# Finishing a cached row one unit earlier in the stick-breaking stage: gather ahead of the scores, weights and value groups moved up

## The chip, the cores and the metric

The kernel runs on one core of one Trainium2 chip. The metric is the device time of one launch in microseconds (µs), the median of several executions. The engines are called PE (TensorE), DVE (VectorE), ACT (ScalarE), POOL (GpSimd) and SP (SyncE, here a queue that only issues DMAs). Each engine runs its own list of instructions in order, and waits on semaphores for the others.

## The reference

One layer of a decoder mixes four parallel head groups, for a prompt of 1024 tokens and for 8 sample rows that each have 4096 cached tokens in 32 pages of 128. The part that matters here is group C, stick-breaking attention:

```
def stick_breaking(q, k, v, q_off, logit_bias):
    ...
        z = jnp.einsum('bqhd,bshd->bhqs', qi, kf) * Dh ** -0.5 + bias
        mask = kpos[None, :] < pi[:, None]
        l1mb = jnp.where(mask, jax.nn.log_sigmoid(-z), 0.0)
        after = lax.cumsum(l1mb, axis=3, reverse=True) - l1mb
        A = jnp.where(mask, jnp.exp(jax.nn.log_sigmoid(z) + after), 0.0)
        return jnp.einsum('bhqs,bshd->bqhd', A, vf)
...
        k_past = cache_sb_k[l][page_table].reshape(DB, past, SB_HEADS, SB_DIM)
        v_past = cache_sb_v[l][page_table].reshape(DB, past, SB_HEADS, SB_DIM)
```

For the prompt, queries and keys are the same 1024 tokens. For a sample row there is one query against the 4096 cached keys and values.

## The kernel before

The program is a chain of stages with a barrier between them. The change lies in the stage `stick_breaking_prompt`, which runs from about 110 to 565 µs of the profiled execution and does three things at once.

**The prompt.** The 8 heads are taken as 4 pairs, i = 0 to 3. A pair is cut in 12 pieces, u = 0 to 11, of one block of 128 queries by up to 512 keys: blocks 0 to 3 have one piece each (of 128, 256, 384 and 512 keys), blocks 4 to 7 two. The engines' loops run over g = 12 i + u; one turn is called a unit here. In unit g, PE multiplies the scores of piece g (L699, with the mask L705 on the diagonal), then a third of a projection tile (24 matmuls, L317; the last pair has only three such thirds, in its units 3 to 5), then it transposes the weights of piece g-2 (L717) and multiplies those of piece g-3 with the values (L732). ACT makes `keep` (L498) and `A` (L502) from the scores of each of the two heads; the second head's `keep` stands in ACT's list behind the first head's `A`, which needs a buffer that PE's transposes of unit g-2 set free. DVE scans `keep` to `left` (L567, L571) and multiplies it into `A` (L580).

**Tokens and tiles.** In units 2, 3 and 4 PE also transposes the new values, the sample row's tokens and the keys (L746, L773). DVE copies them out at the head of units 3 (`v_tok`, L623), 4 (`new_tok`, L628) and 5 (`k_tok`, L634), and PE's transposes of weights in these units wait for the copies, since they share the PSUM banks. At the head of unit 3 DVE also does `gate(i - 1, 1)` (L587), on which POOL's `store` (L669) waits.

**The cached rows.** Pair i also carries the sample row i. Its keys were multiplied with the query by POOL (L1966) and reduced by DVE (L1972) during the pair before; each POOL multiply takes a pair of pages, in a ring of four buffers. At the end of unit 11, ACT loads its exp/ln table, does `softplus_tail` (L1986 to L1990) and loads the sigmoid table again (L87), and DVE does `softplus` (L1994). Then, in the pair the row belongs to:

- PE `sum_pages` (L2002, L2003), the sums over the tokens of a page; unit 2
- DVE `exponents` (L2010 to L2018: a copy, a subtraction, 8 scans, a subtraction); unit 2
- ACT `weights` (L2023) between two table loads; unit 3
- PE `values.weigh` (L2096), 8 groups of 8 matmuls, one each at the end of the units 4 to 11 (`GROUPS`); SP loads the values for it (L2083), in a ring of four pairs of pages
- DVE `take_partial` (L2106) of the finished row; end of unit 0 of the next pair
- PE `gather` (L2112, 4 matmuls); unit 1 of the next pair, behind the projection third
- DVE `keep` (L2118); unit 1 of the next pair

SP's list is written by hand: loads of keys, values, weight tiles and stores of tokens alternate in a fixed order, and each waits there for its buffer.

Of the kernel before, what the change touches and what calls it, by code (L numbers as in the profile page):

```python
# [20 lines left out]
GT = GW // P  # L21
# [304 lines left out]
def stick_breaking_prompt(nc, ctx, k):  # L326
# [52 lines left out]
    values = PagedValues(ctx, nc, k, "cp", 0, GT, 4, PARTIAL, page_A)  # L379
# [1 line left out]
    Z, TURN, Y = k.bank[3:5], (k.bank[5], k.bank[2]), k.bank[6]  # L381
    quad = lambda bank: bank[:, :].rearrange("p (b t) -> p b t", b=4)
    REDUCES = (2, 1, 2, 1, 2, 1, 2, 1, 2, 1, 1, 0)
    GROUPS = (4, 5, 6, 7, 8, 9, 10, 11)
    V_TURNED, NEW_TURNED, K_TURNED = 2, 3, 4

    with nc.Block() as block:
# [76 lines left out]
        @block.scalar  # L464
        def _(act):
            keys.setup_scalar(act)

            def take(t, j, c):
                name, i = t
                columns = slice(c * CH, (c + 1) * CH)  # L470
                if name == "V":
                    if c == 0 and i:
                        act.wait_ge(tok_turned, 5 * i - 2)
                    stream.take(act, j, c, vT[:, columns], ACT.Copy)
                if name == "K":
                    if c == 0 and i > 1:
                        act.wait_ge(scored, 2 * NU * (i - 1))
                        act.wait_ge(tok_turned, 5 * (i - 1))
                    stream.take(act, j, c, kT[:, i % 2, columns], ACT.Copy)
                if name == "Q":  # L480
                    if c == 0 and i > 1:
                        act.wait_ge(scored, 2 * NU * (i - 1))
                    stream.take(act, j, c, qT[:, i % 2, columns], ACT.Copy, scale=SCORE_SCALE)
                if name == "G":
                    if i and c < 2:
                        act.wait_ge(mix_out[c], 16 * i)
                    if i and c == 2:
                        act.wait_ge(new_kept, i)
                    act.wait_ge(stream.projected, 3 * j + c + 1)
                    nc.scalar.activation(mix[:, columns], stream.bank(j, c)[:, 0:CH], ACT.Sigmoid).then_inc(gate_open, 1)  # L490

            def sigmoids(n):
                i, q, c = piece(n // 2)
                h, w = n % 2, wide(q, c)
                act.wait_ge(scored, n + 1)
                if n >= RK:
                    act.wait_ge(left_ready, n - RK + 1)
                nc.scalar.activation(keep[:, n % RK, W - w:W], Z[h][:, 0:w], ACT.Sigmoid, scale=-1.0,  # L498
                                     bias=minus[:, 2 * i + h:2 * i + h + 1]).then_inc(keep_ready, 1)
                if n >= RA:  # L500
                    act.wait_ge(A_turned, n - RA + 1)
                nc.scalar.activation(A[:, n % RA, 0:w], Z[h][:, 0:w], ACT.Sigmoid,  # L502
                                     bias=bias[:, 2 * i + h:2 * i + h + 1]).then_inc(sig_ready, 1)

            def take_turned(n):
                i, q, c = piece(n // 2)
                w = wide(q, c)
                act.wait_ge(A_turned, n + 1)
                if n >= RT:
                    act.wait_ge(weighted, n - RT + 1)  # L510
                nc.scalar.activation(AT[:, n % RT, 0:w], TURN[n % 2][:, 0:w], ACT.Copy).then_inc(AT_ready, 1)

            stream.split_hi(act, 0)
            stream.split_hi(act, 1)
            for j in range(3):
                for c in range(3):
                    take(tiles[j], j, c)
                stream.split_hi(act, j + 2)
            load_tables(nc, act, LN_EXP)
            keys.softplus_tail(act, 0)  # L520
            load_tables(nc, act, SIGMOID)
            act.wait_ge(bias_in, 16)
            act.wait_ge(minus_set, 1)
            act.wait_ge(ones_set, 1)
            for g in range(LAST + 3):
                i, u = g // NU, g % NU
                if g < LAST:
                    sigmoids(2 * g)
                    sigmoids(2 * g + 1)
                if g in chunk_of:  # L530
                    take(*chunk_of[g])
                if 2 <= g < LAST + 2:
                    take_turned(2 * g - 4)
                    take_turned(2 * g - 3)
                if u % 3 == 0 and 4 * i + 5 + u // 3 - 1 < len(tiles) and g:
                    stream.split_hi(act, 4 * i + 4 + u // 3)
                if u == 3 and i < GT:
                    load_tables(nc, act, LN_EXP)
                    act.wait_ge(values.weighed.sem, values.weighed.at(i, 0))
                    keys.weights(act, i)  # L540
                    load_tables(nc, act, SIGMOID)
                if u == NU - 1 and i + 1 < GT:
                    load_tables(nc, act, LN_EXP)
                    keys.softplus_tail(act, i + 1)
                    load_tables(nc, act, SIGMOID)

        @block.vector
        def _(dve):
# [65 lines left out]
            keys.softplus(dve, 0)  # L614
            for g in range(LAST + 3):
                i, u = g // NU, g % NU
                if u == V_TURNED + 1:
                    if i:
                        gate(i - 1, 1)
                        dve.wait_ge(v_out, 16 * i)  # L620
                    for q in range(2):
                        dve.wait_ge(tok_turned, 5 * i + q + 1)
                        nc.vector.tensor_copy(v_tok[:, 4 * q:4 * q + 4, :], quad(TURN[q])).then_inc(tok_taken, 1)  # L623
                if u == NEW_TURNED + 1:
                    dve.wait_ge(tok_turned, 5 * i + 3)
                    if i:
                        dve.wait_ge(new_out, 32 * i)
                    nc.vector.tensor_copy(new_tok[:].rearrange("p a b -> p (a b)"), TURN[0][0:NB, 0:2 * P]).then_inc(tok_taken, 1)  # L628
                if u == K_TURNED + 1:
                    if i:  # L630
                        dve.wait_ge(k_out, 16 * i)
                    for q in range(2):
                        dve.wait_ge(tok_turned, 5 * i + q + 4)
                        nc.vector.tensor_copy(k_tok[:, 4 * q:4 * q + 4, :], quad(TURN[q])).then_inc(tok_taken, 1)  # L634
                if u == HALF + 3:
                    gate(i, 0)
                if g < LAST:
                    products_left(2 * g)
                    products_left(2 * g + 1)
                    weights(2 * g)  # L640
                    weights(2 * g + 1)
                if g in chunk_of and chunk_of[g][0][0] == "G":
                    open_gate(chunk_of[g][1], chunk_of[g][2], i)
                if u % 3 == 0 and 4 * i + 4 + u // 3 < len(tiles) and g:
                    stream.split_lo(dve, 4 * i + 4 + u // 3)
                if u == 0 and i:
                    values.take_partial(dve, i - 1)
                if u == 1 and i:
                    values.keep(dve, i - 1)
                if u == 2 and i < GT:  # L650
                    keys.exponents(dve, i)
                if i < GT:
                    reduce_keys(i + 1, REDUCES[u])
                if u == NU - 2 and i + 1 < GT:
                    keys.add_bias(dve, i + 1)
                if u == NU - 1 and i + 1 < GT:
                    keys.softplus(dve, i + 1)
# [28 lines left out]
        def _(pe):  # L686
# [64 lines left out]
                    stream.chunk(pe, j, c)  # L751
            for g in range(LAST + 3):
                i, u = g // NU, g % NU
                if g < LAST:
                    scores(g)
                if g in chunk_of:
                    stream.chunk(pe, *chunk_of[g][1:])
                if u == 1 and i:
                    values.gather(pe, i - 1)
                if u == 2 and i < GT:  # L760
                    if i:
                        pe.wait_ge(values.kept.sem, values.kept.at(i, 0))
                    keys.sum_pages(pe, i)
# [11 lines left out]
                if i < GT and u == K_TURNED:  # L775
                    turn_tokens(kT[:, i % 2, :], tile_of["K", i], 5 * i + 3, g)
                if i < GT and u in GROUPS:
                    if u == GROUPS[0]:
                        pe.wait_ge(keys.A_ready.sem, keys.A_ready.at(i, 1))
                    values.weigh(pe, i, 2 * GROUPS.index(u))  # L780

# [38 lines left out]
class MemoryKeys:  # L820
# [14 lines left out]
    def quad(self):  # L835
        return self.bank[:, :].rearrange("p (b t) -> p b t", b=4)
# [1652 lines left out]
```

## Time and profile before

| | µs |
|---|---|
| Median of 3 executions | 1546.62 (1545.63 to 1547.21) |
| The profiled execution, its own time | 1546.62 |
| Its span in the trace | 1544.6 |
| Scores of pairs 0, 1, 2, 3 begin at (unit 0) | 151.8, 268.5, 375.0, 479.4 |
| PE busy | 1279.8, 83% of the span |
| DVE busy | 862.2, 56% |
| Mean granted clock of PE | 0.904 |

The profile is one execution. Busy shares are averages over the stages; a stage is read from its timelines, which give each instruction's start, its duration and, in brackets, the idle time ahead of it and what ended it. Busy time of DVE and POOL includes time in which an instruction had begun and stood still.

### The profile page before, as it was taken

To read this page: it belongs to the slowest core of one execution; us is meant where nothing else is said; L and a number is where in the kernel's file an instruction comes from. 1 tells how busy PE (TensorE), PEld (TensorE's weight loads), DVE (VectorE), ACT (ScalarE), POOL (GpSimd) and SP (SyncE) were. 2 spreads that over 40 slices of the span, in tenths; PEclk is the share of its full clock that TensorE was granted. 3 is DMA by queue.
4 is the path that set the end of the run, shared out by engine and by line. 5 is a ranking of instruction groups with operands and counts; after the bars stand their busy time and mean duration, and the time that the engine had idled before them with its cause. 6 is when DMAs were issued, how large, how long until landed. Compare 5 with 4: busy or idle time off the path is not lost. (4 is left out here: it accounts for less than half of the span.)

```text
span 1544.6 us, 23117 instructions
## 1 busy us (share of the span) xinstructions
PE 1279.8 (83%) x7719; PEld 1070.4 (69%) x7719; DVE 862.2 (56%) x1198; ACT 484.5 (31%) x902; POOL 358.3 (23%) x235
## 2 busy tenths in 40 slices
PE   3549589889798864998988899599999997797997
PEld 2539457767676543888888888488777776466885
DVE  4434779889886532759779496243434443324221
ACT  5311245435445531242232413231313131322110
POOL 0027544424330000736434354000000000000000
PEclk8679799999898986999999999798999997798999
DMA  4536657557473423655354642575646452543320
GB/s 137 164 91 213 199 183 248 169 176 248 141 228 110 146 81 103 209 172 177 104 170 140 206 150 71 163 217 154 205 143 215 141 178 70 177 136 109 109 81 28
DMA packets 200420, 237.89 MB, mean 154 GB/s; under 512 B 13539, under 2 KB 122434, under 8 KB 200298
## 3 DMA queue, kind: packets, MB, share of 16 engines
q1 hardware_dynamic: 196338, 224.61, 46.8%
q0 software_dynamic: 3968, 11.87, 2.1%
q8 instruction: 59, 0.97, 0.3%
q14 instruction: 55, 0.45, 0.1%
HBM read 215.88 MB, written 20.64 MB: 153 GB/s over the span
## 5 line engine op out<-in xcount | busy, mean ns | idle before, releaser
L1966 POOL TENSOR_TENSOR cp_keys<-cp_keys,cp_q 128x1024 f32<-128x1024 f32 x64 | 162.0, 2548 | 156.9 <-DMA cp_keys<-cache_sb_k 156.5
L1966 POOL TENSOR_TENSOR bp_keys<-bp_keys,bp_q 128x1024 f32<-128x1024 f32 x64 | 156.8, 2471 | 166.9 <-DMA bp_keys<-cache_sb_k 159.1
L248 PE MATMUL bank<-xh,b_w_hi 128*128 128x344 f32 x480 | 162.7, 339 | 31.4 <-DVE b_w_lo L231 27.2
L248 PE MATMUL bank<-xl,b_w_hi 128*128 128x344 f32 x480 | 157.8, 329 | 0.0
L248 PE MATMUL bank<-xh,b_w_lo 128*128 128x344 f32 x480 | 157.6, 328 | 0.0
L248 PE MATMUL bank<-xh,d_w_hi 128*128 128x344 f32 x384 | 131.1, 341 | 25.0 <-DVE d_w_lo L231 17.4
L317 PE MATMUL bank<-xh,c_w_hi 128*128 128x344 f32 x384 | 129.4, 337 | 17.0 <-DVE c_w_lo L303 17.0
L248 PE MATMUL bank<-xl,d_w_hi 128*128 128x344 f32 x384 | 126.2, 329 | 0.0
L317 PE MATMUL bank<-xl,c_w_hi 128*128 128x344 f32 x384 | 126.2, 329 | 0.0
L248 PE MATMUL bank<-xh,d_w_lo 128*128 128x344 f32 x384 | 126.1, 328 | 0.0
L317 PE MATMUL bank<-xh,c_w_lo 128*128 128x344 f32 x384 | 125.9, 328 | 0.0
L248 PEld LDWEIGHTS bank<-xh,b_w_hi 128*128 128x128 f32 x480 | 94.6, 197 | 34.7 <-ACT b_w_hi L226 28.0
L567 DVE TENSOR_TENSOR_SCAN c_left<-c_keep,ones 128x128 f32<-128x128 f32 (+3 forms) x64 | 98.7, 1557 | 33.1 <-ACT c_keep L498 32.9
L248 PEld LDWEIGHTS bank<-xh,d_w_hi 128*128 128x128 f32 x384 | 75.3, 196 | 53.2 <-issue 39.3
L2332 PE MATMUL bank<-o_w_hi,o_mix_hi 128*128 128x512 f32 x256 | 102.8, 401 | 10.5 <-DVE o_raw L2286 8.6
L502 ACT ACTIVATE c_A<-bank,c_bias 128x512 f32<-128x512 f32 (+3 forms) x96 | 55.8, 581 | 148.3 <-PE bank L717 148.3
L2332 PE MATMUL bank<-o_w_lo,o_mix_hi 128*128 128x512 f32 x256 | 101.6, 397 | 0.0
L2332 PE MATMUL bank<-o_w_hi,o_mix_lo 128*128 128x512 f32 x256 | 101.4, 396 | 0.0
L1972 DVE TENSOR_REDUCE bp_page_z<-bp_keys 128x16 f32<-128x1024 f32 x64 | 75.2, 1213 | 36.2 <-POOL bp_keys L1966 36.2
L248 PEld LDWEIGHTS bank<-xl,b_w_hi 128*128 128x128 f32 x480 | 94.4, 197 | 1.5 <-issue 1.4
L317 PEld LDWEIGHTS bank<-xh,c_w_hi 128*128 128x128 f32 x384 | 75.5, 197 | 27.1 <-issue 27.1
L248 PEld LDWEIGHTS bank<-xh,b_w_lo 128*128 128x128 f32 x480 | 94.0, 196 | 0.0
(381 smaller groups left out, 2600.1 us busy)
## 6 DMA issues: line engine op xcount, KB each, us to landing
cp_keys<-cache_sb_k SPq DMA_DIRECT2D x128, 256.0 KB, 2.9
cp_values<-cache_sb_v SPq DMA_DIRECT2D x128, 256.0 KB, 2.8
bp_keys<-cache_sb_k SPq DMA_DIRECT2D x128, 256.0 KB, 3.2
dp_values<-cache_sb_v SPq DMA_DIRECT2D x128, 256.0 KB, 2.9
b_w_raw<-w_in SPq DMA_DIRECT2D x20, 512.0 KB, 4.2
c_w_raw<-w_in SPq DMA_DIRECT2D x16, 512.0 KB, 5.1
d_w_raw<-w_in SPq DMA_DIRECT2D x16, 512.0 KB, 5.2
o_mix<-mix SPq DMA_DIRECT2D x8, 1024.0 KB, 5.8
```

The source lines that it names most:

```text
L248: last = self.nc.tensor.matmul(self.bank(j, c)[:, 0:self.width], w[:, s, k, :], x[:, k, c * self.width:(c + 1) * self.width], start=(k == ...
L317: last = self.nc.tensor.matmul(self.bank(j, c)[:, 0:self.width], w[:, k, :], x[:, k, columns], start=(k == 0 and m == 0), stop=(k == KT - ...
L502: nc.scalar.activation(A[:, n % RA, 0:w], Z[h][:, 0:w], ACT.Sigmoid, bias=bias[:, 2 * i + h:2 * i + h + 1]).then_inc(sig_ready, 1)
L567: nc.vector.tensor_tensor_scan(left[:, n % RL, W - w:W][:, ::-1], keep[:, n % RK, W - w:W][:, ::-1], k.ones512[:, 0:w], 1.0, ALU.mult, ALU ...
L1966: self.nc.gpsimd.tensor_tensor(self.keys[:, s], self.keys[:, s], q, ALU.mult).then_inc(self.scaled.sem, 1)
L1972: self.nc.vector.tensor_reduce(self.z[:, i % 2, :, 2 * r:2 * r + 2].rearrange("p h r -> p r h"), self.keys[:, r % self.ring].rearrange("p ...
L2332: last = nc.tensor.matmul(ACC[b][h][:, :], m[:, b, kk, :], w[:, kk, h * H:(h + 1) * H], start=(kk == 0 and n == 0), stop=(kk == KO - 1 and ...
```

## The change

The work on a cached row ends a unit earlier. `take_partial` goes to the head of unit 0 on DVE, ahead of its scans; `gather` goes to the head of unit 0 on PE, ahead of the scores; `keep` goes to unit 0. `sum_pages` and `exponents` move from unit 2 to unit 1, `weights` with its two table loads from unit 3 to unit 2. The eight value groups lie in units 3 to 6 and 8 to 11, unit 7 has none. SP's list is not changed. The loops also run three turns past the last unit, so the last row's `take_partial` and `gather` move with the others: ahead of the last transposes and weighings.

```
-    GROUPS = (4, 5, 6, 7, 8, 9, 10, 11)
+    GROUPS = (3, 4, 5, 6, 8, 9, 10, 11)
...
-                if u == 3 and i < GT:
+                if u == 2 and i < GT:
                     load_tables(nc, act, LN_EXP)
                     act.wait_ge(values.weighed.sem, values.weighed.at(i, 0))
                     keys.weights(act, i)
...
             for g in range(LAST + 3):
                 i, u = g // NU, g % NU
+                if u == 0 and i:
+                    values.take_partial(dve, i - 1)
                 if u == V_TURNED + 1:
...
                 if u == 0 and i:
-                    values.take_partial(dve, i - 1)
-                if u == 1 and i:
                     values.keep(dve, i - 1)
-                if u == 2 and i < GT:
+                if u == 1 and i < GT:
                     keys.exponents(dve, i)
...
             for g in range(LAST + 3):
                 i, u = g // NU, g % NU
+                if u == 0 and i:
+                    values.gather(pe, i - 1)
                 if g < LAST:
                     scores(g)
                 if g in chunk_of:
                     stream.chunk(pe, *chunk_of[g][1:])
-                if u == 1 and i:
-                    values.gather(pe, i - 1)
-                if u == 2 and i < GT:
+                if u == 1 and i < GT:
                     if i:
                         pe.wait_ge(values.kept.sem, values.kept.at(i, 0))
                     keys.sum_pages(pe, i)
```

## Rows read from the trace of the kernel before

**Rows 1.** Window, unit 7 of pair 1: length, busy PE, PEld, DVE, ACT, POOL; clock; DMA.

```profile
335.00:342.40 7.40, 7.34 (x52) 5.26 (x48) 7.40 (x9) 3.34 (x6) 1.59 (x3) 1.00 0.81 238
```

**Rows 2.** Waits of the stage, 150 to 560: who waited for whom, us, times, longest.

```profile
PEld bank L717 <- DVE c_new_tok L628: 17.3, 3, 6.4
```

**Rows 3.** Timeline of all engines where pair 0 ends and pair 1 begins.

```profile
268.54 0.49 PE L699 MATMUL bank<-c_kT,c_qT 64*128 64x128 f32 x4
...
271.22 0.42 DVE L1994 SCALAR_TENSOR_TENSOR cp_page_L<-cp_page_z,cp_page_soft 128x256 f32<-128x256 f32 x1
```

**Rows 4.** TensorE's timeline: unit 1 of pair 1, units 0 of pairs 2 and 3, unit 1 of pair 3.

```profile
279.80 0.95 PE L2112 MATMUL bank<-ones,cp_y_rows 128*128 128x1 f32 x8
...
374.97 0.49 PE L699 MATMUL bank<-c_kT,c_qT 64*128 64x128 f32 x4
...
479.35 0.49 PE L699 MATMUL bank<-c_kT,c_qT 64*128 64x128 f32 x4
...
485.53 1.22 PE L699 MATMUL bank<-c_kT,c_qT 64*128 64x256 f32 x4 [3.33 <-ACT c_A L502]
```

**Rows 5.** VectorE's and ScalarE's timelines at the borders of pairs 2 and 3.

```profile
378.21 0.42 DVE L1994 SCALAR_TENSOR_TENSOR cp_page_L<-cp_page_z,cp_page_soft 128x256 f32<-128x256 f32 x1
...
483.05 0.42 DVE L1994 SCALAR_TENSOR_TENSOR cp_page_L<-cp_page_z,cp_page_soft 128x256 f32<-128x256 f32 x1 [2.05 <-ACT cp_page_soft L1990]
...
485.10 0.38 ACT L502 ACTIVATE c_A<-bank,c_bias 128x128 f32<-128x128 f32 x1
```

**Rows 6.** VectorE's timeline, units 2 and 3 of pair 1.

```profile
291.63 0.42 DVE L2010 COPY cp_page_L<-bank 128x256 f32<-128x256 f32 x1
...
293.69 2.34 DVE L1972 TENSOR_REDUCE cp_page_z<-cp_keys 128x16 f32<-128x1024 f32 x2
295.95 0.68 DVE L587 TENSOR_TENSOR c_mix<-bank,c_mix 128x512 f32<-128x512 f32 x1
...
297.74 11.63 DVE L567 TENSOR_TENSOR_SCAN c_left<-c_keep,ones 128x512 f32<-128x512 f32 x2
```

**Rows 7.** GpSimd's timeline, 284 to 307.

```profile
284.42 2.39 POOL L1966 TENSOR_TENSOR cp_keys<-cp_keys,cp_q 128x1024 f32<-128x1024 f32 x1 [8.09 <-DMA cp_keys<-cache_sb_k]
...
297.86 9.30 POOL L1966 TENSOR_TENSOR cp_keys<-cp_keys,cp_q 128x1024 f32<-128x1024 f32 x4
```

**Rows 8.** TensorE's timeline, units 2 to 4 of pair 1; the last row unit 4 of pair 2.

```profile
287.80 0.38 PE L2002 MATMUL bank<-cp_page_L,from_here 128*128 128x256 f32 x1
288.01 0.59 PE L2003 MATMUL bank<-cp_page_L,ones 128*128 128x256 f32 x2
...
300.97 0.37 PE L773 MATMUL bank<-ident,c_kT 128*8 128x128 f32 x1 [2.06 <-ACT c_AT L511]
...
313.62 1.54 PE L717 MATMUL bank<-ident,c_A 128*128 128x128 f32 x6 [5.12 <-DVE c_new_tok L628]
...
420.04 1.54 PE L717 MATMUL bank<-ident,c_A 128*128 128x128 f32 x6 [6.11 <-DVE c_new_tok L628]
```

**Rows 9.** The end of the stage: TensorE's timeline, then VectorE's.

```profile
552.47 1.12 PE L717 MATMUL bank<-ident,c_A 128*128 128x128 f32 x8 [0.29 <-ACT c_AT L511]
...
554.53 1.05 PE L2112 MATMUL bank<-ones,cp_y_rows 128*128 128x1 f32 x8
...
553.68 0.69 DVE L2106 TENSOR_TENSOR cp_y_rows<-bank,cp_own 128x512 f32<-128x512 f32 x1
```

**Rows 10.** TensorE's value groups that waited for a load: pair 1 unit 9; pair 3 unit 8.

```profile
357.50 1.04 PE L2096 MATMUL bank<-cp_values,c_page_A 128*8 128x512 f32 x8 [1.00 <-DMA cp_values<-cache_sb_v]
...
537.92 1.07 PE L2096 MATMUL bank<-cp_values,c_page_A 128*8 128x512 f32 x8 [2.65 <-DMA cp_values<-cache_sb_v]
538.93 2.08 PE L699 MATMUL bank<-c_kT,c_qT 64*128 64x512 f32 x4
```

**Rows 11.** Window over the end of unit 3 and most of unit 4, pair 1; columns as above.

```profile
299.90:306.70 6.80, 5.73 (x22) 5.11 (x23) 6.80 (x1) 5.76 (x9) 6.80 (x4) 0.50 0.46 156
```

More of the change, by code:

```diff
@@ L383, in stick_breaking_prompt @@
     REDUCES = (2, 1, 2, 1, 2, 1, 2, 1, 2, 1, 1, 0)
-    GROUPS = (4, 5, 6, 7, 8, 9, 10, 11)
+    GROUPS = (3, 4, 5, 6, 8, 9, 10, 11)
     V_TURNED, NEW_TURNED, K_TURNED = 2, 3, 4
@@ L536, in _ @@
                     stream.split_hi(act, 4 * i + 4 + u // 3)
-                if u == 3 and i < GT:
+                if u == 2 and i < GT:
                     load_tables(nc, act, LN_EXP)
@@ L616, in _ @@
                 i, u = g // NU, g % NU
+                if u == 0 and i:
+                    values.take_partial(dve, i - 1)
                 if u == V_TURNED + 1:
@@ L646, in _ @@
                 if u == 0 and i:
-                    values.take_partial(dve, i - 1)
-                if u == 1 and i:
                     values.keep(dve, i - 1)
-                if u == 2 and i < GT:
+                if u == 1 and i < GT:
                     keys.exponents(dve, i)
@@ L753, in _ @@
                 i, u = g // NU, g % NU
+                if u == 0 and i:
+                    values.gather(pe, i - 1)
                 if g < LAST:
@@ L757, in _ @@
                     stream.chunk(pe, *chunk_of[g][1:])
-                if u == 1 and i:
-                    values.gather(pe, i - 1)
-                if u == 2 and i < GT:
+                if u == 1 and i < GT:
                     if i:
```

## The prediction

> **What bounds the kernel now.** I read the page first, then the waits of the stage, then the timelines of its borders. The page makes TensorE the busiest engine. In an undisturbed unit the reader is to see it busy for 7.34 of 7.40 µs at the full clock [rows 1], with VectorE occupied as long, part of it standing still. So the stage goes by TensorE, except where something stops it. The timelines show two such kinds of place in each pair.
>
> The first is unit 4. TensorE stands still for 5.12 µs in pair 1 and 6.11 µs in pair 2, and each time it is VectorE's copy of the new tokens that releases it [rows 8]; the waits give 17.3 µs for this wait over three pairs [rows 2]. VectorE is late because of unit 3: two scans of 512 take 11.63 µs, and beside them lie four multiplies of GpSimd in one piece, 297.86 to 307.16 [rows 6, 7]. VectorE gets on only when GpSimd pauses. GpSimd has four at once because its list waited for VectorE's gate at 295.95. From the gate to the end of TensorE's stall is 313.62 - 295.95 = 17.7 µs, of fixed steps; in pair 2 it is the same to 0.1. So in pairs 1 and 2 the time of the gate sets the time of all that follows. Its own time follows from TensorE's unit 2 and VectorE's work there.
>
> The second is not seen yet. At the border of two pairs TensorE runs on into unit 0 at 268.54, 374.97 and 479.35, while VectorE is still at `softplus` of the new row, which ends at 271.64, 378.63 and 483.47 [rows 3 to 5]. VectorE is 3.1 to 4.1 µs behind, because ScalarE's two table loads stand ahead of that instruction. Nobody suffers from it today.
>
> **The change part by part.**
>
> *Gather at the head of unit 0.* PE can't score before it has gathered, gather waits for `take_partial`, and that is behind `softplus`. After the end of `softplus` come 0.69 for `take_partial`, 0.16 to the first matmul of gather and about 0.9 for gather [rows 9], less a little overlap on VectorE: 1.7 µs. The scores of unit 0 then start at 271.64 + 1.7 = 273.3 instead of 268.54 (4.8 late), at 380.3 instead of 374.97 (5.4 late) and at 485.2 instead of 479.35. Behind gather are queued the scores, the projection third, the transposes and so all that ScalarE and VectorE get. The delay is not taken up on the way: units 0 to 2 are paced by TensorE's transposes, which ScalarE's second `keep` waits for. In pair 3 there is almost no projection, and unit 1 waited for ScalarE until 485.53 anyway [rows 4]. There, 0.9 for the scores and about 1.2 for ScalarE's four small sigmoids (0.38 each, overlapping) [rows 5] follow 485.2: unit 1 at 487.3, some 1.7 late.
>
> *Gather out of unit 1, the page sums in.* 0.95 leaves and 288.60 - 287.80 = 0.80 comes [rows 4, 8]: no change for unit 1.
>
> *Page sums and exponents out of unit 2.* The sums stood ahead of the transposes that the second scan hangs on: 0.8 earlier. The exponents took 293.69 - 291.63 = 2.06 of VectorE ahead of the gate [rows 6]. So the gate comes up to 2.9 earlier after the start of unit 2, and by the fixed 17.7 so does the end of the stall. Against it: in unit 1 the exponents would run about 8.4 to 10.5 µs after its start (275.06 for pair 1), and a multiply of GpSimd starts at 284.42, 9.4 after it [rows 7]. It can hold scans up to 2.4 µs, of which VectorE's later wait for `keep` takes up all but about 0.7. I take 2.5, between 2.2 and 2.9.
>
> The SBUF page of the Trainium skill ("two separate sides") says that VectorE and GpSimd share a port pair as an exclusive lock, held for the whole instruction by the one that starts first. The rows agree that it is all or nothing, but not on the length: the first scan begins 0.12 ahead of the multiplies and lasts through four of them. By one instruction of lock the stall of unit 4 would hardly be there.
>
> *Weights with table loads to unit 2.* Some 3 µs of ScalarE now lie ahead of its first `keep` of unit 3, about 1 µs more than it was idle there. VectorE wants that `keep` only after gate and copies, which hide it: nothing. If that cover went, about 1 µs a pair.
>
> *A value group in unit 3, none in unit 7.* The group, 1.0 µs [rows 10], lies ahead of the stall of unit 4, in its cover, in pairs 0 to 2. Pair 3 has no such stall, so +1.0. In unit 7 TensorE would wait for ScalarE's last `A` anyway: 0, and in the short units of pair 3 -0.5. SP's loads of values wait for the groups and come earlier for all but the last two, which ends waits of 1.00 in pair 1 and 2.65 in pair 3, and behind the latter the scores that ran at the low clock (2.08 for 1.13) give 0.9 [rows 10]. The waits in unit 11 lie ahead of the new stall and give nothing.
>
> *The end.* Gather now stands ahead of the last transposes of weights. It can't start before 554.53, as `take_partial` is still VectorE's next work at 553.68; the transposes that ran at 552.47 begin near 555.45: 3.0 late, less the 0.9 that gather no longer takes further on: +2.1 [rows 9]. The last gate, store and stage end follow.
>
> *Clock.* TensorE stands still for some 3.8 µs at each border. After an idle of 2.06 in unit 3 the granted clock was 0.50, the level of 1.2 GHz, from 299.9 to 306.7 [rows 8, 11]. Such a stretch on dense work costs half its length, at most 3.4; part of it falls in the idle itself. I take 1.7 for borders 1 and 2, bounds 0 and 3.4. At border 3 the clock was low already. The page "TensorE: Matmul & The Clock Gate" of the Trainium skill (Part 1) has the array fall to half rate after idling; the rows agree, and by that rule the new idle is not free, which speaks against the change.
>
> *Sum.* Pair 0: 0, as its unit 3 waits for keys that SP sends late, which the change doesn't move. Pair 1: 4.8 - 2.5 - 1.0 + 1.7 = +3.0. Pair 2: 5.4 - 2.5 + 1.7 = +4.6. Pair 3: 1.7 - 0.8 (sums out of unit 2) + 1.0 - 0.5 - 2.65 - 0.9 + 2.1 = -0.1. In all +7.5: 1546.6 + 7.5 = 1554.1. The profiled execution took 1546.62, as the median does, with a span of 1544.6.
>
> **Rivals.**
>
> *A: the border gets worse.* Loads come earlier, so GpSimd's multiplies move too. If one falls on VectorE's scans in unit 11, `softplus` and with it gather come 2.4 µs later. For it: GpSimd has multiplies near each of these borders. Against: today none of them delays `softplus`. Over two or three borders +5 to +7: near 1560.
>
> *B: it evens out.* The clock doesn't fall, the exponents meet no multiply, and pair 0 gives up to 2.9 as well since its exponents leave unit 2 too. 1554.1 - 3.4 - 0.8 - 2.9 = 1547.0. Against: each border's wait is hard.
>
> *C: the scan of unit 3 escapes.* The collision hangs on 0.12 µs. If the first scan gets through before GpSimd's four multiplies, the two stalls of 5.12 and 6.11 go: 1554.1 - 11.2 = 1542.9, faster. It decides from the point where the scan starts one length (1.2 µs) ahead. For it: VectorE is less loaded. Against: gate, copies, store and scan follow one another exactly as before, so both move together.
>
> **How the numbers follow.** My forecast's own range is 1554.1 - 3.4 - 0.8 = 1549.9 to 1554.1 + 3.4 + 0.6 = 1558.1. Chances: forecast 0.52, A 0.18, B 0.19, C 0.11. The range leaves out C and the top of A: 1546 to 1561. A measurement of this kernel tells 0.2%, about 3 µs, from no change: slower is the forecast and A, 0.70; within it B, 0.19; faster C, 0.11.
>
> **What would show it.** TensorE waiting for VectorE's `take_partial` ahead of gather, 3.5 to 4.5 µs at each of three borders, and the clock at half behind it; the gate 10.4 to 11.1 µs after unit 2's start instead of 13.3; the stall of unit 4 still there, with scans of some 11 µs; no waits for values in pair 3; gather ahead of the last transposes. I am wrong if TensorE reaches gather no earlier than VectorE is done, or if the piece of four multiplies breaks up.

## The result: slower by 1.2%, more than twice what was forecast

| | Before | Changed |
|---|---|---|
| Median, µs | 1546.35 (1545.63 to 1547.21, 4 runs) | 1566.54 (1564.60 to 1567.64, 4 runs) |
| Ratio, 95% interval | | 1.0118 [1.0096, 1.0142] |
| Span of the profile | 1544.6 | 1561.4 |
| Next stage's first matmul (L248) | 572.8 | 585.6 |

The changed kernel was measured once more, beside the kernel before on the same chip (e10): 1567.11 against 1546.82, ratio 1.0106 [1.0066, 1.0146]. The forecast was 1554.1 with a range up to 1561.

In the waits of the stage, 150 to 571, the wait for the partial row takes 24.4 µs in all, where the kernel before had 0.2; the columns are the time waited, how often, and the longest:

```profile
PEld bank L2112 <- DVE cp_y_rows L2106: 24.4, 4, 9.3
...
PE bank L2112 <- DVE cp_y_rows L2106: 20.7, 4, 8.4
```

These are four waits of TensorE (and of its weight loads, PEld) ahead of gather, for VectorE's `take_partial`: at the three borders of two pairs and at the end of the stage. This is the wait that was forecast, but longer. The timeline of all engines at the border of pairs 0 and 1 shows it, and answers to [rows 3]:

```profile
264.89 1.04 PE L2096 MATMUL bank<-cp_values,c_page_A 128*8 128x512 f32 x8
...
265.39 2.46 DVE L571 TENSOR_TENSOR_SCAN c_left<-c_keep,c_left,ones 128x513 f32<-128x513 f32 x2
...
267.67 5.09 POOL L1966 TENSOR_TENSOR cp_keys<-cp_keys,cp_q 128x1024 f32<-128x1024 f32 x2 [4.94 <-DMA cp_keys<-cache_sb_k]
267.77 5.55 DVE L580 TENSOR_TENSOR c_A<-c_A,c_left 128x512 f32<-128x512 f32 x2
...
273.24 0.41 DVE L1994 SCALAR_TENSOR_TENSOR cp_page_L<-cp_page_z,cp_page_soft 128x256 f32<-128x256 f32 x1
273.57 0.68 DVE L2106 TENSOR_TENSOR cp_y_rows<-bank,cp_own 128x512 f32<-128x512 f32 x1
...
274.31 1.87 PE L2112 MATMUL bank<-ones,cp_y_rows 128*128 128x1 f32 x8 [8.37 <-DVE cp_y_rows L2106]
...
276.10 0.80 PE L699 MATMUL bank<-c_kT,c_qT 64*128 64x128 f32 x4
```

The reader is to see three things. TensorE has done its last group at 265.93 and idles 8.37 µs. VectorE's two multiplies of `A` (L580) take 5.55 µs where they take 1.27 alone, beside two multiplies of GpSimd, the first of which starts 0.1 µs ahead of them: this is 4.3 µs for VectorE and, since it would have had to wait for ScalarE a little anyway, 3.7 µs for gather. And gather itself takes 1.87 instead of 0.95 [rows 4]; the granted clock is at its lower level there (0.50 from 274.31 to 276.10). The window over most of unit 0 behind it, with the mean granted clock as the seventh value (0.58), then DMA:

```profile
276.10:283.70 7.60, 7.60 (x33) 7.35 (x33) 0.42 (x1) 0.37 (x1) 0.00 (x0) 0.58 0.13 46
```

Unit 0 of pair 1 takes 9.40 µs (276.10 to 285.50) instead of 6.52. TensorE's timeline at border 3, where no multiply of GpSimd is near, shows the wait at its shortest, 4.72:

```profile
489.44 1.04 PE L2096 MATMUL bank<-cp_values,c_page_A 128*8 128x512 f32 x8
495.20 1.87 PE L2112 MATMUL bank<-ones,cp_y_rows 128*128 128x1 f32 x8 [4.72 <-DVE cp_y_rows L2106]
497.00 0.80 PE L699 MATMUL bank<-c_kT,c_qT 64*128 64x128 f32 x4
...
498.21 1.93 PE L717 MATMUL bank<-ident,c_A 128*128 128x128 f32 x8
...
501.52 0.70 PE L699 MATMUL bank<-c_kT,c_qT 64*128 64x256 f32 x4
```

The gains came as forecast. VectorE's timeline of units 2 and 3 of pair 1, against [rows 6], and TensorE's stall, against [rows 8]; unit 2 began at 293.09:

```profile
301.88 2.34 DVE L1972 TENSOR_REDUCE cp_page_z<-cp_keys 128x16 f32<-128x1024 f32 x2
304.13 0.68 DVE L587 TENSOR_TENSOR c_mix<-bank,c_mix 128x512 f32<-128x512 f32 x1
...
305.92 11.65 DVE L567 TENSOR_TENSOR_SCAN c_left<-c_keep,ones 128x512 f32<-128x512 f32 x2
```

```profile
321.82 1.54 PE L717 MATMUL bank<-ident,c_A 128*128 128x128 f32 x6 [4.62 <-DVE c_new_tok L630]
```

The gate comes 11.04 after the start of unit 2 instead of 13.32; from the gate to the end of the stall it is 17.7 again, with the two scans at 11.65, as good as unchanged (11.63).

### The profile page after: what moved, and what is told of

Its sections match the earlier page's. It is cut to its first block and busy times, and to the rows that moved or that the text cites. A ratio compares the mean times of both kernels' runs of the same rounds, so it can differ in the third digit from the quotient of the medians.

```text
span 1561.4 us, 23117 instructions
## 1 busy us (share of the span) xinstructions
PE 1282.6 (82%) x7719; PEld 1072.4 (69%) x7719; DVE 857.7 (55%) x1198; ACT 484.5 (31%) x902; POOL 359.5 (23%) x235
## 5 line engine op out<-in xcount | busy, mean ns | idle before, releaser
L248 PE MATMUL bank<-xh,b_w_hi 128*128 128x344 f32 x480 | 163.6, 341 | 31.3 <-DVE b_w_lo L231 27.2
L248 PE MATMUL bank<-xl,b_w_hi 128*128 128x344 f32 x480 | 158.5, 330 | 0.0
L248 PE MATMUL bank<-xh,b_w_lo 128*128 128x344 f32 x480 | 157.8, 329 | 0.0
L248 PE MATMUL bank<-xh,d_w_hi 128*128 128x344 f32 x384 | 130.7, 340 | 26.1 <-ACT d_w_hi L226 18.4
L248 PE MATMUL bank<-xl,d_w_hi 128*128 128x344 f32 x384 | 125.7, 327 | 0.0
L248 PE MATMUL bank<-xh,d_w_lo 128*128 128x344 f32 x384 | 125.7, 327 | 0.0
L248 PEld LDWEIGHTS bank<-xh,b_w_hi 128*128 128x128 f32 x480 | 94.9, 198 | 34.6 <-ACT b_w_hi L226 28.0
L248 PEld LDWEIGHTS bank<-xh,d_w_hi 128*128 128x128 f32 x384 | 74.9, 195 | 54.2 <-issue 40.4
L2332 PE MATMUL bank<-o_w_hi,o_mix_hi 128*128 128x512 f32 x256 | 103.0, 402 | 10.5 <-DVE o_raw L2286 8.6
L567 DVE TENSOR_TENSOR_SCAN c_left<-c_keep,ones 128x128 f32<-128x128 f32 (+3 forms) x64 | 79.1, 1257 | 44.2 <-ACT c_keep L498 44.1
L248 PEld LDWEIGHTS bank<-xl,b_w_hi 128*128 128x128 f32 x480 | 94.9, 198 | 1.6 <-issue 1.5
L248 PEld LDWEIGHTS bank<-xh,b_w_lo 128*128 128x128 f32 x480 | 94.6, 197 | 0.0
```

The lines of the kernel that those rows point to most:

```text
L248: last = self.nc.tensor.matmul(self.bank(j, c)[:, 0:self.width], w[:, s, k, :], x[:, k, c * self.width:(c + 1) * self.width], start=(k == ...
L567: nc.vector.tensor_tensor_scan(left[:, n % RL, W - w:W][:, ::-1], keep[:, n % RK, W - w:W][:, ::-1], k.ones512[:, 0:w], 1.0, ALU.mult, ALU ...
L2332: last = nc.tensor.matmul(ACC[b][h][:, :], m[:, b, kk, :], w[:, kk, h * H:(h + 1) * H], start=(kk == 0 and n == 0), stop=(kk == KO - 1 and ...
```

## The experiments

Each profile is read by the starts of the scores (L699). With `take_partial` behind `softplus`, gather never started sooner than 12.5 µs after the start of unit 11; that is called the floor. "Stage end" is the next stage's first matmul less its 572.8 in the kernel before; the times have that kernel beside them on the same chip.

| | Gather starts after start of unit 11, borders 1, 2, 3 | Stage end | Ratio of times, 95% interval |
|---|---|---|---|
| Changed | 16.1, 13.1, 12.5 | +12.8 | 1.0118 [1.0096, 1.0142] |
| Changed again (e10) | 13.6, 17.4, 12.5 | +16.0 | 1.0106 [1.0066, 1.0146] |
| e1 gather behind the third | inside unit 0 | +0.6 | 1.0013 [0.9990, 1.0036] |
| e2 gather only | 14.4, 12.5, 12.5 | +13.9 | 1.0118 [1.0082, 1.0154] |
| e3 last gather back | 13.5, 13.4, 12.5 | +8.6 | 1.0077 [1.0046, 1.0108] |
| e4 delay, kernel before | | +11.1 | 1.0078 [1.0048, 1.0108] |
| e5 gather at end of unit 0 | inside unit 0 | -17.2 | 0.9932 [0.9909, 0.9955] |
| e5 again (e12) | inside unit 0 | -6.3 | 0.9946 [0.9927, 0.9966] |
| e6 e5, partial before softplus | inside unit 0 | -14.0 | 0.9926 [0.9898, 0.9954] |
| e7 e5, weights and groups back | inside unit 0 | -9.3 | 0.9980 [0.9957, 1.0003] |
| e8 the wait filled | 16.2, 17.9, 12.5 | +17.7 | 1.0065 [1.0044, 1.0086] |
| e9 keys behind values | 12.5, 12.5, 12.5 | +9.7 | 1.0060 [1.0035, 1.0084] |
| e11 before again | | -1.2 | 0.9998 [0.9980, 1.0015] |

**e1: is it the place of gather?**

```
                     stream.chunk(pe, *chunk_of[g][1:])
+                if u == 0 and i:
+                    values.gather(pe, i - 1)
```

(and it goes from ahead of the scores.)

> The changed kernel, but in unit 0 TensorE does the scores and the projection third first and gathers behind them; VectorE's take_partial stays at the head of unit 0, the page sums, exponents, weights and value groups stay moved up. Theory (the border): what makes the changed kernel slow is TensorE standing still ahead of unit 0 for VectorE's take_partial. Then the stalls of borders 1 and 2 go (scores of unit 0 about 1 us or less behind the end of unit 11 instead of 10.2 and 7.1 us), the earlier gates stay, and the kernel is 4 to 8 us faster than the kernel before, some 25 us faster than the changed one; pair 3 and the end of the stage, which have no third in unit 0, keep most of their loss. Rival (the moved groups, weights and exponents cost the time themselves): it stays above the kernel before by 10 us or more.

The loss went, 12 µs at the stage's end against the changed kernel's first profile, but the kernel before was not beaten, where 4 to 8 µs were expected. The profile shows why: at border 2 the wait only moved. Gather began 8.64 after the scores of unit 0, with the third done at 4.69, since VectorE was held by GpSimd once more, and unit 0 took 12.95 µs. In pair 3 there is no third in unit 0 and gather still stood ahead of the transposes; counted from the start of unit 0, unit 1 came 4.1 later. The theory of the border holds; a third is too little cover. TensorE's gather at border 2:

```profile
380.82 1.05 PE L2112 MATMUL bank<-ones,cp_y_rows 128*128 128x1 f32 x8 [3.95 <-DVE cp_y_rows L2106]
```

**e2: the gather alone.** The kernel before with `take_partial`, `gather` and `keep` moved as in the change, nothing else.

> The kernel before with only take_partial, gather and keep moved to unit 0, take_partial and gather at its head; page sums, exponents, weights and value groups as before. Theory (the border): all of the loss and none of the gains, so slower than the changed kernel: 20 to 25 us above the kernel before. The border's wait of pair 1 is some 2 us shorter than in the changed kernel if GpSimd's multiplies fall on VectorE's unit 11 only because the value groups and with them SP's loads come earlier. Rival (moved groups and exponents cost the time): 0 to 6 us above the kernel before.

It is as slow as the whole change, with groups, exponents and weights where they were: the rival is out. It was not slower than the whole change as expected, 16 µs by the medians instead of 20 to 25. At border 1 gather starts at 14.4, 1.7 sooner than in the changed kernel's first profile but beyond the floor of 12.5, though no load moved. Here `softplus` itself (L1994, 0.42 alone) took 2.38 beside a multiply of GpSimd that began 0.25 ahead of it:

```profile
268.66 4.83 POOL L1966 TENSOR_TENSOR cp_keys<-cp_keys,cp_q 128x1024 f32<-128x1024 f32 x2 [5.66 <-DMA cp_keys<-cache_sb_k]
...
268.91 2.38 DVE L1994 SCALAR_TENSOR_TENSOR cp_page_L<-cp_page_z,cp_page_soft 128x256 f32<-128x256 f32 x1 [0.20 <-ACT cp_page_soft L1990]
```

So the collision is possible without earlier loads. How often it comes with them and without is counted where the prediction is answered below.

**e3: the end of the stage.** The changed kernel with `gather` at `g == LAST` back behind `weigh`.

> The changed kernel with the last row's gather alone back where it was at the end of the stage: behind the transposes and weighings of the turn after the last unit. Theory: the end of the stage gets back what the gather and the low clock behind it took there, so 3 to 5 us faster than the changed kernel. Rival: the end of the stage is set by something else, within 1 us of the changed kernel.

From the scores of the last unit to the end of the last weighing it is 11.2 µs again (556.71 to 567.95), where the changed kernel takes 16.4 (555.82 to 572.17). The changed kernel's timeline:

```profile
562.01 1.53 PE L2112 MATMUL bank<-ones,cp_y_rows 128*128 128x1 f32 x8 [2.25 <-DVE cp_y_rows L2106]
563.40 1.95 PE L717 MATMUL bank<-ident,c_A 128*128 128x128 f32 x8
565.28 1.98 PE L732 MATMUL bank<-c_AT,c_v_tok 128*64 128x128 f32 x16
567.18 1.99 PE L717 MATMUL bank<-ident,c_A 128*128 128x128 f32 x8
```

and with the last gather back:

```profile
560.94 1.12 PE L717 MATMUL bank<-ident,c_A 128*128 128x128 f32 x8 [0.30 <-ACT c_AT L511]
561.99 1.09 PE L732 MATMUL bank<-c_AT,c_v_tok 128*64 128x128 f32 x16
563.01 1.05 PE L2114 MATMUL bank<-ones,cp_y_rows 128*128 128x1 f32 x8
563.92 1.07 PE L717 MATMUL bank<-ident,c_A 128*128 128x128 f32 x8
```

From the scores of the last unit to the next stage it is 24.7 µs, against 29.8 and 28.5 in the two profiles of the changed kernel: 5.1 and 3.8 less, where 3 to 5 were expected; by the ratios the kernel is 4 to 6 µs faster than the changed one. Of the 5.1 the wait and the place of gather are some 2, and the rest goes with the low clock, at which gather, transposes and weighings took up to 1.99 for 1.12; this split is an estimate from the rows above.

**e4: do the stages behind care when they start?** Seven memsets of VectorE behind the last gate of the kernel before.

> The kernel before with seven VectorE memsets of 128x2052 (1.8 us each) behind the last gate of the stick-breaking stage; nothing else changed and the output is the same. It asks where the some 4 us come from that the changed kernel loses behind this stage, in stages whose code is the same. Theory (they depend on the instant at which they start): the later stages also take 1 to 5 us more or less than in the kernel before. Rival (they do not): from the next stage's first matmul on, all is later by one constant, about 9 us, within 0.5 us.

The next stage began 11.1 later, the last matmul only 9.2: from one to the other 959.1 µs, against 961.0. That is 1 to 5 µs of difference, as the theory had it, but e11 and e12 below show that two profiles of one kernel can differ there by more; so e4 does not show that the start is the cause.

**e5: the gather where nobody waits.**

```
                 if g >= 3:
                     weigh(g - 3)
+                if u == 0 and i:
+                    values.gather(pe, i - 1)
```

(and it goes from ahead of the scores; all else as in the change.)

> The changed kernel with gather at the end of unit 0 on TensorE, behind the third, the transposes and the weighing, at all three borders and at the end of the stage; all else stays moved up. Theory (TensorE must not want the partial row before VectorE has it): no wait of several us for take_partial at any border, even where GpSimd's multiplies hold VectorE; unit 5 of pairs 1 and 2 comes 3 us earlier per pair as in the changed kernel; pair 3 and the end of the stage lose nothing. The stage ends 8 to 13 us earlier than in the kernel before, the time is 0.5 to 0.9% below it. Rival (the earlier gates only look like a gain and are given back): within 3 us of the kernel before.

This beats both kernels: 0.9932, and 0.9946 when run again. Border 1 in TensorE's timeline:

```profile
265.25 1.04 PE L2096 MATMUL bank<-cp_values,c_page_A 128*8 128x512 f32 x8
266.23 0.49 PE L699 MATMUL bank<-c_kT,c_qT 64*128 64x128 f32 x4
...
271.72 1.09 PE L732 MATMUL bank<-c_AT,c_v_tok 128*64 128x128 f32 x16
...
272.75 1.05 PE L2112 MATMUL bank<-ones,cp_y_rows 128*128 128x1 f32 x8
273.73 0.70 PE L699 MATMUL bank<-c_kT,c_qT 64*128 64x256 f32 x4
```

The scores follow the last group at once, gather takes 1.05 and ends no wait at this border; at border 3, where unit 0 has no third, gather still waited 1.9. The expected stage end (8 to 13 earlier) was too careful for this execution, with 17.2; but its profile is of the fastest of the executions, 1527.0 where the median is 1536.8.

**e12: e5 again.**

> The kernel of e5_gather_end_of_unit0 once more, unchanged. Its first profile was of its fastest execution (1527), with the stage ending 17 us earlier than before, while its median was only 10 us below. Theory: a typical execution ends the stage 12 to 17 us earlier and the stages behind differ by chance by some us; the ratio of times lies at 0.990 to 0.996 again. Rival (the first measurement was luck): the interval reaches 1.

The ratio is right, the stage end is not: only 6.3 earlier. Its border 2 shows that the wait was not gone for good:

```profile
376.75 1.09 PE L732 MATMUL bank<-c_AT,c_v_tok 128*64 128x128 f32 x16
380.86 1.63 PE L2112 MATMUL bank<-ones,cp_y_rows 128*128 128x1 f32 x8 [3.02 <-DVE cp_y_rows L2106]
```

VectorE can be held so long that even all of unit 0 doesn't cover it; units 0 and 1 of pair 2 then took 6.2 µs more than in e5's profile, clock included.

**e6: the partial row ahead of softplus.** `take_partial(dve, i)` at the end of unit 11, ahead of `softplus`, else as e5.

> As e5_gather_end_of_unit0, and VectorE does take_partial at the end of unit 11 ahead of softplus instead of behind it. Theory: nobody waits for take_partial in e5 any more, so it changes nothing that can be measured: within 2 us of e5. Rival (softplus a little later delays the page sums, or TensorE still waited for take_partial): 2 us or more to either side.

Within 1.3 µs of e5 by the medians (1535.5 and 1536.8), as expected. Whether it shuts out the wait of e12 one profile can't say; it had none.

**e7: the exponents alone.** e5 with `GROUPS` and the weights as before; the page sums and exponents stay in unit 1.

> As e5_gather_end_of_unit0 with the weights back in unit 3 and the value groups back in units 4 to 11: what is left of the change is the exponents and page sums in unit 1 and the finished row one unit earlier. It asks where the gain comes from. Theory: about 3 us in each of pairs 1 and 2 from the earlier gate, by the exponents alone; the waits for values of pair 1 (1 us) and pair 3 (3 us and the low clock behind it) come back, so 3 to 5 us slower than e5. Rival (the groups' order is worth nothing): within 1.5 us of e5 at the end of the stage.

0.9980 against 0.9932: the moved groups and weights are worth about 6 µs by the medians, somewhat more than the expected 3 to 5. The waits for values are back: 1.9 and 1.6 in unit 11 of pairs 0 and 1, and in pair 3 units 7 to 9 take 15.5 µs together, where e5 takes 11.0. Pairs 1 and 2 keep the earlier gate (unit 2 to unit 5: 33.7 and 33.3, before 37.5 and 37.3).

**e8: the price of the low clock.**

```
+                if u == 0 and i and i < GT:
+                    pe.wait_ge(sig_ready, 2 * g)
+                    for n in range(5):
+                        nc.tensor.matmul(Z[0][:, 0:W], k.ident[:], k.ones512[:, 0:W], start=True, stop=True)
```

> The changed kernel with five idle matmuls of 128x512 into a free scores bank ahead of each of the three gathers in pairs 1 to 3 (their result is overwritten by the scores), so that TensorE is not idle while it waits for take_partial; the output is the same. It prices the low clock at the border by itself. Theory: the wait still ends with take_partial, but gather takes 1.0 instead of 1.9 us and unit 0 behind it 6.5 instead of 8.2 to 9.4 us in pairs 1 and 2: 2.5 to 3.8 us a border, 6 to 9 us in all below the changed kernel. Rival (the clock is not what makes unit 0 long): within 2 us of the changed kernel, or slower by the matmuls that outlast the wait.

At border 3, where the wait is at its floor, the five matmuls just fill it:

```profile
497.97 4.56 PE L757 MATMUL bank<-ones,ident 128*128 128x512 f32 x10
502.76 1.05 PE L2116 MATMUL bank<-ones,cp_y_rows 128*128 128x1 f32 x8 [0.23 <-DVE cp_y_rows L2110]
503.75 0.49 PE L699 MATMUL bank<-c_kT,c_qT 64*128 64x128 f32 x4
...
506.46 0.70 PE L699 MATMUL bank<-c_kT,c_qT 64*128 64x256 f32 x4
```

Gather takes 1.05 for 1.87 and unit 0 2.71 for 4.52: the low clock costs 2.6 µs at a border, with the wait the same. At borders 1 and 2 the waits were so long (8.5 and 9.8 µs) that the filling ended 4.0 and 5.3 µs ahead of gather, and gather ran at 1.87 and 1.86 again; the price of the clock can't be read there, and the stage ended no earlier than the changed kernel's. By the ratios it is 1.0065 against 1.0118 and 1.0106, 6 to 8 µs better, which agrees with the expected 6 to 9; but the intervals of e8 and e10 overlap, and the profile accounts for 2.6 of it alone.

**e9: is it GpSimd that lengthens the wait?** Two entries of SP's list exchanged, in the changed kernel:

```
+                load_values(i + 1, 0, 4)
                 load_keys(i + 2, 2, 4)
-                load_values(i + 1, 0, 4)
```

> The changed kernel with two entries of SP's list exchanged at the end of a pair: the loads of key pages 2 and 3 of the row after next stand behind the first four value loads instead of ahead of them, so GpSimd's two multiplies of these pages come some 8 us later and no longer fall into VectorE's unit 11. Theory (what lengthens the wait ahead of gather beyond its floor is GpSimd holding VectorE ahead of take_partial): gather starts 12.5 us after unit 11's start at borders 1 and 2, as it does at border 3, with no VectorE instruction held between the scans of unit 11 and take_partial. In the changed kernel it was 16.1 and 13.1. Rival (the excess has another cause, such as ScalarE or the value groups): it stays at 13 to 16 at one of them.

All three borders are at 12.47. Border 1:

```profile
265.99 2.46 DVE L571 TENSOR_TENSOR_SCAN c_left<-c_keep,c_left,ones 128x513 f32<-128x513 f32 x2
268.36 1.27 DVE L580 TENSOR_TENSOR c_A<-c_A,c_left 128x512 f32<-128x512 f32 x2
269.99 0.42 DVE L1994 SCALAR_TENSOR_TENSOR cp_page_L<-cp_page_z,cp_page_soft 128x256 f32<-128x256 f32 x1 [0.36 <-ACT cp_page_soft L1990]
...
271.08 1.87 PE L2112 MATMUL bank<-ones,cp_y_rows 128*128 128x1 f32 x8 [4.54 <-DVE cp_y_rows L2106]
```

L580 takes 1.27 and L1994 0.42, as alone; what is left is the wait for ScalarE's `softplus_tail`. On the same chip the kernel is 9.3 µs faster than the changed one by the medians (1557.8 and 1567.1), 7 by the ratios. It is still 0.6% slower than the kernel before: that is what the floor and the low clock cost without any collision, less the gains.

**e10: the changed kernel again.**

> The changed kernel once more, unchanged, beside e9 on the same chip: how far its border waits and the stages behind differ from one execution to the next. Theory: border 3 at 12.5 us again, as no multiply is left there; borders 1 and 2 anywhere from 12.5 to 18, since the multiplies meet VectorE by chance; the stages behind differ by some us from the first profile with no cause in the change. Rival (the waits are fixed by the program): 16.1 and 13.1 again within 0.3.

Border 2, all engines, the worst of them:

```profile
381.87 5.65 POOL L1966 TENSOR_TENSOR cp_keys<-cp_keys,cp_q 128x1024 f32<-128x1024 f32 x2 [4.39 <-DMA cp_keys<-cache_sb_k]
381.90 3.41 DVE L580 TENSOR_TENSOR c_A<-c_A,c_left 128x512 f32<-128x512 f32 x2
385.24 2.55 DVE L1994 SCALAR_TENSOR_TENSOR cp_page_L<-cp_page_z,cp_page_soft 128x256 f32<-128x256 f32 x1
387.72 0.68 DVE L2106 TENSOR_TENSOR cp_y_rows<-bank,cp_own 128x512 f32<-128x512 f32 x1
...
388.45 1.87 PE L2112 MATMUL bank<-ones,cp_y_rows 128*128 128x1 f32 x8 [9.60 <-DVE cp_y_rows L2106]
```

This time border 1 has 13.6 and border 2 has 17.4: the same program, other collisions.

**e11: the kernel before again.**

> The kernel before once more, unchanged, with a profile of its own. It asks how far the stages behind the stick-breaking stage differ between two executions of one kernel. Theory (the 4 to 5 us that both profiles of the changed kernel lose there are chance, not the change): the stretch from the next stage's first matmul to the last one differs by 2 us or more from the first profile of the kernel before, while the stick-breaking stage itself ends within 2 us. Rival: both agree within 1 us.

From the next stage's first matmul to the end of the last one the two profiles of the kernel before agree exactly, 961.0 and 961.0, so the rival's words came true. But the two profiles of e5's kernel (e5 and e12) have 958.6 and 966.7, and over all fourteen profiles it goes from 957.7 to 966.7.

## Why the prediction was wrong

**Right: what bounds the stage, and the direction.** The waits sat where they were forecast, `take_partial` was released by `softplus` and `softplus` by ScalarE's tables; where nothing disturbs it, gather starts 12.47 after unit 11's start, and the working gave 483.47 + 0.69 + 0.16 - 471.67, less the overlap, 12.6. The signs that would have shown a wrong reading did not come: TensorE waited 4.7 µs or more at every border, and the piece of four multiplies stayed whole.

**Wrong: the border's term.** It was 4.8 and 5.4 for the late scores and 1.7 for the clock, 6.5 and 7.1 in all. Measured, from unit 11's start to unit 1's, against the kernel before: border 1 +11.9 and +8.9 in the two profiles, border 2 +8.0 and +13.4. There are two causes, each with an experiment of its own:

- *The low clock.* It also slows gather itself, by 0.9, which the term left out, and unit 0 behind it took 1.7 to 2.9 longer than before: 2.6 to 3.8 a border for a term of 1.7. e8 measures 2.6 in all at border 3, where the working had said that the clock was low already and counted nothing. It was not yet low: unit 0 of pair 3 began in the kernel before at full clock (1.00 up to 484.2), and unit 1 ran at half.
- *GpSimd's multiplies.* This was rival A, with a chance of 0.18 and a price of 2.4 a border. It happened at both borders in both profiles of the changed kernel, by 0.6 to 4.9 µs beyond the floor, and e9 takes it away by moving the multiplies. The step that failed is the forecast's use of "today none of them delays `softplus`" as a reason to give the collision no part of the border's term.

Two things in the record go against that sentence. First, the multiplies were just behind. In the kernel before, at border 2, one began with `softplus`, and this time VectorE got through in 0.42 and GpSimd's multiply, the first of two, took longer (2.71 for 2.36). An earlier pair of multiplies had already held two `L580` in unit 11, for 5.61 in place of 1.27, so that `softplus` began 0.4 later than where ScalarE alone would let it (11.82 after unit 11's start, 11.38 in e9):

```profile
367.27 5.32 POOL L1966 TENSOR_TENSOR cp_keys<-cp_keys,cp_q 128x1024 f32<-128x1024 f32 x2 [5.33 <-DMA cp_keys<-cache_sb_k]
367.53 5.61 DVE L580 TENSOR_TENSOR c_A<-c_A,c_left 128x512 f32<-128x512 f32 x2
...
378.17 5.16 POOL L1966 TENSOR_TENSOR cp_keys<-cp_keys,cp_q 128x1024 f32<-128x1024 f32 x2 [5.58 <-DMA cp_keys<-cache_sb_k]
```

Second, the change moves them, as rival A said. In the kernel before SP begins to issue the keys in question, at border 1, 6.7 µs after the start of unit 11 (259.63), and in the changed one 4.8 µs after it (258.19):

```profile
266.29 3.12 SPq L1958 DMA_DIRECT2D cp_keys<-cache_sb_k  x4
```

```profile
263.03 3.12 SPq L1958 DMA_DIRECT2D cp_keys<-cache_sb_k  x4
```

The multiply of these keys begins 11.1 to 12.9 after unit 11's start in the five profiles with the groups as before (before, e2, e4, e7, e11), and of ten borders it held `softplus` at one, e2's. It begins 9.3 to 10.8 after it in the eight profiles with the groups moved (all others but e9), and there `softplus` ended late at all sixteen, by 0.5 to 5.5 µs. So the collision comes with the moved groups and weights, which no run takes apart from each other. How much it costs differs between executions of one program, and one profile doesn't price it.

**Wrong: border 3 and the end.** Border 3 was put at 1.7; it cost 4.9 and 5.3 up to unit 1, since gather and the unit's transposes and weighings ran at the low clock; with the wait filled (e8) it cost 2.3. The end was put at +2.1; it was +5.2 and +3.9, and in e3 it is +0.1. Against them pair 3 gained more than forecast from unit 1 to unit 11: -8.4 instead of -3.9. Of this 4.8 lie in units 1 and 2: unit 1 and the start of unit 2 ran at a granted clock of 0.50 before, and both units at 1.00 now. The low clock moved from them to unit 0.

**Right in size: the gains.** The gate came 2.3 earlier after unit 2's start in pair 1, and unit 5 by 3.0 and 3.4 after unit 2's in pairs 1 and 2 (expected 2.5); the wait of unit 9 went (1.0); unit 7 without its group was not shorter in pairs 1 and 2. In pair 1 a multiply of GpSimd held the `L580` ahead of the exponents (2.92 for two), a meeting that was allowed for. e7 shows the earlier gate by itself.

**The sum.** +7.5 was forecast; the stage ended 12.8 and 16.0 later. Without the collisions the forecast would have stood, as far as e9 can tell, which also moves a load: it is 11.0 µs above the kernel before by the medians (9.3 by the ratio), inside the forecast's own range of +3.3 to +11.5. The medians of the changed kernel and the kernel before differ by 20, though, and both profiles of the changed kernel have 4 to 5 µs more behind the stage (965.0 and 966.2 against 961.0); e9 has 965.0 too. The code there is the same, and e5's two profiles differ there by 8.2. So this part is not fixed by the kernel; why the profiles of the changed one, and its medians, fall on the long side stays open. Nor can a single profile price the collisions: between two profiles of one kernel the stage's end differs by 3.2 (changed) and 10.9 (e5).

On the lock: the Trainium skill's page "SBUF — State Buffer" (two separate sides) has the loser wait for one whole instruction of the other. At the borders the traces fit that: in e10 L1994, at 2.55 for 0.42, began 0.5 behind a multiply and ended 0.3 behind it. In unit 3 they do not: the first scan, begun about 0.1 ahead of the multiplies, stands through four of them and takes 10.5 in pairs 1 and 2 of all fourteen profiles. By one instruction it would be done some 7 µs earlier (three multiplies of 2.36; an estimate), and the stall of unit 4, 4.62 above, would hardly be there.

## What to carry to other kernels

Before an engine that bounds the kernel is made to wait for another, look at what the other one does just then and how far behind it is; a lag that costs nothing today has no row in the waits. Ask too what else the change moves near that place: work on a third engine that lies 1 µs behind the critical instruction today may lie on it tomorrow. Price the wait with the low clock behind it, and take one profile's collisions as one draw out of many. Leave a whole unit of cover instead of a third of one; even that was too little once (e12). Here the same change with the gather one unit's work further down turned 1.2% slower into 0.6% faster.

## What the runs showed of the hardware

- After an idle of 4.7 µs TensorE's next unit of short matmuls took 4.52 instead of 2.71, and the four small matmuls of gather 1.87 instead of 1.05, at the same work and at a mean granted clock of 0.56 for 1.00 in the unit; with matmuls of no use in the gap both were at the full rate. Filling was worth 2.6 µs at this border (e8, border 3). At the two borders where the filling ended 4 µs or more too soon gather took 1.87 all the same.
- An instruction of VectorE with two SBUF operands that is held by a GpSimd multiply ends just behind it, whatever its own length: L1994 took 2.38 and 2.55 for 0.42 (e2, e10), two L580 5.55 for 1.27 (changed). Not every meeting holds it: in the kernel before, at border 2, L1994 began 0.04 behind the recorded start of a multiply and took 0.42, and the multiply 2.71 for 2.36. L2106, which reads one of its operands from PSUM, took its 0.68 beside a multiply begun 0.25 ahead of it (e10, border 1: 272.67).
- Which instructions meet changes from one execution to the next: gather at one border began 16.1 and 13.6 after unit 11's start in two executions of one program, at the next 13.1 and 17.4.
